# A two-block transformer kernel: input and norm columns laid out by the host, first two weight slabs taken together by pieces, and several waits and orders moved

## The reference, cut to what matters

```python
hn = rmsnorm(h, norm_mix_g[l])            # h = x, (256, 1024)
proj = hn @ w_in[l]                        # split into fq fk fv ff gq gf gi gg
fox_out = fox_attention(fq, fk, fv, log_sigmoid(ff + fox_f_bias))
rec = hgrn2_chunkwise(gq, gf, gi, lbs[l])  # linear recurrence, gated by gg
h = h + concat(fox_out, rec * ...) @ w_out[l]
mem_n = rmsnorm(mem, norm_mem_g[l])
h = h + memory_cross_attention(rmsnorm(h, norm_x_g[l]), mem_n, w_xq, w_xkv, w_xo)
h = h + square(relu(rmsnorm(h, norm_ff_g) @ w1)) @ w2
h = rmsnorm(h, final_norm_g)
```

## Time and profile before

| | us |
|---|---|
| median of 3 runs | 907.87 (906.85 to 908.96) |
| the profiled execution, whole | 906.91 |
| its span | 905.1 |
| TensorE busy in it | 890.8 (98%) |
| VectorE busy | 605.0 |
| ScalarE busy | 489.3 |

### The profile page before, as it was taken

How to read it: one execution, slowest core, us unless ns; L and a number is a source line. 1 busy time by engine, 2 the same in 40 slices (tenths; PEclk the granted TensorE clock), 3 DMA queues, 4 the chain that set the end, 5 groups by cost and what they waited for, 6 DMA issues and landing times.

```text
span 905.1 us, 15854 instructions
## 1 busy us (share of the span) xinstructions
PE 890.8 (98%) x6305; PEld 820.6 (91%) x6305; DVE 605.0 (67%) x812; ACT 489.3 (54%) x727; POOL 107.6 (12%) x136
## 2 busy tenths in 40 slices
PE   9999999899999999999999999999999999999997
PEld 8988987788988999988899989999999899999886
DVE  6795875755655766644467547898686688888643
ACT  7766545534655655433364336664644666666432
POOL 6431132200000100000026070001000100000000
PEclk9999999999999999999999999999999999999999
DMA  9958632234533866555547554345556486666641
GB/s 290 304 176 278 213 124 94 94 135 144 187 94 94 262 200 202 194 186 189 199 149 224 199 196 150 105 146 158 187 186 186 117 226 192 185 187 203 213 140 47
DMA packets 135266, 159.63 MB, mean 176 GB/s; under 512 B 3951, under 2 KB 113773, under 8 KB 134957
## 3 DMA queue, kind: packets, MB, share of 16 engines
q1 hardware_dynamic: 133261, 151.79, 52.4%
q0 software_dynamic: 1344, 6.03, 1.9%
q10 hardware_dynamic: 608, 1.06, 0.3%
HBM read 157.81 MB, written 1.05 MB: 176 GB/s over the span
## 4 chain that ended last, share of the span: by engine, by line
PE 86%; DVE 5%; ACT 3%; issue 3%; DMA 1%; SPq 1%; POOL 0%; DVEq 0%; POOLq 0%; ACTq 0%
PE tb L698 15%; PE tb L700 15%; PE tb L699 15%; PE acc L698 11%; PE acc L700 11%; PE acc L699 11%; DMA raw<-in_w_in 1%; PE acc L990 1%; ACT whi L1327 1%; DVE wlo L1863 1%; DVE wlo L1939 1%; PE tb L1084 0%; DVE dz L2017 0%; PE acc L1210 0%; PE tb L1066 0%
## 5 line engine op out<-in xcount | busy, mean ns | idle before, releaser
L1863 DVE TENSOR_TENSOR wlo<-raw,whi 128x2048 fp32r<-128x2048 f32 x138 | 317.1, 2301 | 187.6 <-ACT whi L1327 187.2
L1327 ACT ACTIVATE whi<-raw 128x2048 fp32r<-128x2048 f32 x138 | 264.1, 1915 | 183.9 <-PE acc L700 121.5
L698 PE MATMUL tb<-xhi,whi 128*128 128x256 f32 x1192 | 331.8, 278 | 2.1 <-DVEq L2002 1.2
L700 PE MATMUL tb<-xhi,wlo 128*128 128x256 f32 x1192 | 329.3, 276 | 0.0
L699 PE MATMUL tb<-xlo,whi 128*128 128x256 f32 x1192 | 329.3, 276 | 0.0
L698 PEld LDWEIGHTS tb<-xhi,whi 128*128 128x128 f32 x1192 | 223.8, 188 | 3.0 <-DVEq L2002 1.4
L699 PEld LDWEIGHTS tb<-xlo,whi 128*128 128x128 f32 x1192 | 223.9, 188 | 0.1
L700 PEld LDWEIGHTS tb<-xhi,wlo 128*128 128x128 f32 x1192 | 223.8, 188 | 0.0
L698 PE MATMUL acc<-whi,hid_hi 128*128 128x512 f32 x128 | 50.0, 390 | 0.0
L700 PE MATMUL acc<-whi,hid_lo 128*128 128x512 f32 x128 | 49.8, 389 | 0.0
L699 PE MATMUL acc<-wlo,hid_hi 128*128 128x512 f32 x128 | 49.8, 389 | 0.0
(11 more groups left out here) (408 smaller groups left out, 1524.2 us busy)
## 6 DMA issues: line engine op xcount, KB each, us to landing
raw<-in_w_in SPq DMA_DIRECT2D x37, 1024.0 KB, 5.2
raw<-in_w SPq DMA_DIRECT2D x32, 1024.0 KB, 5.4
raw<-in_w_up SPq DMA_DIRECT2D x44, 512.0 KB, 5.0
raw<-in_w_down SPq DMA_DIRECT2D x22, 512.0 KB, 4.1
raw<-in_w_xkv SPq DMA_DIRECT2D x8, 1024.0 KB, 6.3
raw<-in_w_out SPq DMA_DIRECT2D x8, 1024.0 KB, 4.9
raw<-in_w_mem_kv SPq DMA_DIRECT2D x4, 1024.0 KB, 5.1
raw<-in_w_xq SPq DMA_DIRECT2D x4, 1024.0 KB, 5.0
```

The source lines that it names most:

```text
L698: pe.matmul(o, a_hi, b_hi, start=start, stop=False)
L700: return pe.matmul(o, a_lo, b_hi, start=False, stop=stop)
L1327: act.activation(whi[:, n % RING, :m], raw[:, n % RING, :m], ACT.Copy).then_inc(hi_ready, 1)
L1863: dve.tensor_tensor(low(n), raw[:, n % RING, :m], whi[:, n % RING, :m].bitcast(F32), ALU.subtract).then_inc(lo_ready, 1)
```

## The change: the input and the norm columns from the host, a new opening, orders and waits moved

- The host lays out x transposed (`xT`), all small parameters as 128-row columns (`cols`), and the first six slabs as they lie in SBUF (`opening`, 8 KB per partition and slab). Two DMAs bring `cols` (64 B, later 952 B, per partition) in place of 15; PE's turning of x and of the columns goes, with `turn_x`.
- SP loads, for each of four g: x^T piece g (256 KB), piece g of slab 0, piece g of slab 1; then slab 2, then x (for the sums alone). ACT and DVE split x^T straight from SBUF (`x_hi`, `x_lo`), and PE takes slabs 0 and 1 together, piece by piece (`first_pair`).
- ACT: the sums of x come after both banks of slabs 0 and 1 are emptied and before the pieces of slab 3. The sums of `mem` and their load come later; `laid` of `mem` and `spread("mem")` move to `fv`. `spread("x")` moves from behind slab 2 to between the pieces of slab 3.
- Slab 6 gets bank 3 and waits for no bank. `lo` of slab 8 goes ahead of the scans on DVE, and slab 5's bank and `hi` of slab 8 ahead of ACT's Exp and Ln.
- Around heads 5 and 7, `vm`, `xo`, `plo` and `h4` the orders change as below.

```diff
-            load_x(0)
-            load_x(2)
-            load_piece(0, 0)
-            load_x(1)
-            load_x(3)
+            for g in range(4):
+                sp.dma_start(turned_x[:, 2 * g:2 * g + 2, :], w["xT"][:, 2 * g:2 * g + 2, :]).then_inc(xT_in[g], 16)
+                load_piece(0, g)
+                load_piece(1, g)
+            for p in range(PIECES[2]):
+                load_piece(2, p)
+            for q in range(4):
+                load_x(q)
...
-        X_BANK = {0: 0, 1: 1, 2: 2, 3: 0, 4: 1, 5: 0, 6: 1, 7: 0, 8: 1}
-        BANK_BEFORE = {3: 0, 4: 1, 5: 3, 6: 4, 7: 5, 8: 6}
+        X_BANK = {0: 0, 1: 1, 2: 2, 3: 0, 4: 1, 5: 0, 6: 3, 7: 0, 8: 1}
+        BANK_BEFORE = {3: 0, 4: 1, 5: 3, 7: 5, 8: 4}
...
+            def first_pair():
+                for p in range(4):
+                    for n in range(2):
+                        if p == 3:
+                            split_ready(n)
+                        else:
+                            pe.wait_ge(piece_hi, 2 * p + n + 1)
+                            pe.wait_ge(piece_lo, 2 * p + n + 1)
+                        pe.wait_ge(xs["lo"], p + 1)
+                        for c in range(2):
+                            for k in (2 * p, 2 * p + 1):
+                                last = mm3(o, a_hi[n][:, k, m], a_lo[n][:, k, m], XHI["x"][:, k, :], XLO["x"][:, k, :],
+                                           k == 0, k == 7)
...
                 empty_pair(A + j, dz[:, 0, d:d + T], dz[:, 0, d + T:d + 2 * T])
-                if j:
-                    act.wait_ge(mem_in, 16)
-                    sumsq("mem", xn)
+            for q in range(4):
+                act.wait_ge(x_in[q], 16)
+                sumsq("x", h, [q])
+            for j in range(2):
                 for p in range(2):
                     hi_piece(A + j + RING, p)
...
@@ ACT, 12 slabs
+                if i in (5, 7):
+                    fox_copy(i - 1)
+                if i == 5:
+                    hi(n + RING)
                 if i == 7:
-                    fox_copy(6)
+                    laid(turned_mem, C["norm_mem_2"], (2, 3))
+                    fox_exp(7)
+                    hg_exp(8)
+                    fox_hi(6)
@@ PE, 12 slabs, i == 7
                         emptied(first["xk"] + 3)
-                        emptied(first["xv"] + 3)
@@ DVE, 12 slabs
-                if i == 7:
-                    laid(turned_mem, C["norm_mem_2"], (2, 3), 4)
-                lo(n + RING)
-                if i == 7:
-                    hg_diff(8)
+                if i not in (7, 11):
+                    lo(n + RING)
                 if i < 8:
                     fox_mask(i)
+                    if i == 7:
+                        laid(turned_mem, C["norm_mem_2"], (2, 3), 4)
+                        hg_diff(8)
...
+                    if i == 7:
+                        lo(n + RING)
...
+                    dve.wait_ge(slab_done, n + 1)
+                    dve.tensor_scalar(vm[:, 1, :], acc[:, 0, 1, :], rs[:, NORM["mem2"], 1:2], None, ALU.mult).then_inc(vm_low, 1)
...
-            h4_lo(0, (0, 1))
+            h4_lo(0, (0,))
             summed("h4", 1)
+            h4_lo(0, (1,))
```

More of the change, by code:

```diff
@@ L467, in _ @@
-            load_x(2)
-            load_piece(0, 0)
-            load_x(1)
-            load_x(3)
[L471 to L477, removed]
+                sp.dma_start(raw[:, n % RING, cut], w["opening"][n, :, cut]).then_inc(landed_at, 16)
@@ L481, in _ @@
[L481 to L486, removed]
@@ L751, in row_slab @@
                             last.then_inc(part_done, 1)
-                last.then_inc(slab_done, 1)
+                if tiles[-1]:
+                    last.then_inc(slab_done, 1)
             def tile_slabs(n0, hi, lo, k0):
@@ L903, in _ @@
             A = first["gf"]
-            for n in range(A, first["fv"]):
+            first_pair()
+            for n in range(A + 2, first["fv"]):
                 if n in BANK_BEFORE:
                     emptied(BANK_BEFORE[n])
-                if n == 1:
-                    filled("x")
                 if n in PIECES:
@@ L912, in _ @@
                     t_slab(n, XHI["x"], XLO["x"], X_BANK[n])
[L913 to L927, removed]
+            emptied(2)
+            pe.wait_ge(spread_kept, 1)
             for j, name in enumerate(("fv", "gi", "gg")):
@@ L932, in _ @@
                     half_slab(first[name] + k, XHI["x"], XLO["x"], 4 * k, j % 2)
+                if name == "fv":
+                    spread("mem", tb[:, 2, :])
             def fox_scores(i):
@@ L1401, in hi_piece, with x_hi @@
                     .then_inc(hi_ready if p == PIECES[n] - 1 else piece_hi, 1)
[L1403 to L1408, removed]
+            def x_hi(g):
+                act.wait_ge(xT_in[g], 16)
+                for kt in (2 * g, 2 * g + 1):
+                    last = act.activation(XHI["x"][:, kt, :], turned_x[:, kt, :], ACT.Copy,
                                           scale=cols[:, C["norm_mix_g"] + kt:C["norm_mix_g"] + kt + 1])
-                last.then_inc(fil["hi"], 1)
+                last.then_inc(xs["hi"], 1)
             def empty_pair(n, one, two, scale=1.0):
@@ L1416, in empty_pair @@
                 act.activation(two, second_bank(n), ACT.Copy, scale=scale).then_inc(act_emptied, 1)
-            act.wait_ge(cols_ready, 1)
+            act.wait_ge(cols_in["first"], 16)
             for g in range(4):
-                turn_x(g)
+                x_hi(g)
                 hi_piece(0, g)
[L1422 to L1425, removed]
+                hi_piece(1, g)
             for p in range(2):
@@ L1476, in _ @@
             hi(n + RING)
+            act.wait_ge(mem_in, 16)
+            sumsq("mem", xn)
             for j in range(2):
@@ L1483, in _ @@
                 hi(n - 1 + RING)
+                if name == "fv":
+                    act.wait_ge(cols_ready, 1)
+                    act.wait_ge(memT_in, 16)
+                    laid(turned_mem, C["norm_mem_g"], range(4))
+                else:
+                    act.wait_ge(spread_made, 2)
+                    act.activation(factor_r, tb[:, 2, 0:T], ACT.Copy).then_inc(spread_kept, 1)
                 empty(n, dst[:, 0, :], ACT.Copy, acc[:, j, 0, :], scale=rs[:, NORM["x"], 0:1])
@@ L2039, in _ @@
             link(dve.tensor_scalar(small[:, 56:57], small[:, 56:57], -LAM_INIT, None, ALU.add))
-            lo(first["fq"] + 2 + RING)
-            laid(turned_mem, C["norm_mem_g"], range(4), 0)
-            for n in range(first["fq"] + 3, first["gg"] + 1):
+            for n in range(first["fq"] + 2, first["gg"] + 1):
                 lo(n + RING)
+                if n == first["fv"]:
+                    laid(turned_mem, C["norm_mem_g"], range(4), 0)
             def hg_diff(m):
```

160 lines of the change are left out of this document (75 added, 85 removed).

## The result

The changed kernel takes 902.23 us, the median of five runs (901.81 to 904.0); the kernel before took 907.87 (906.85 to 908.96). The ratio is 0.9945, 95% interval [0.9932, 0.9959]. Forecast were 901.3 and 898.0 to 904.5. The time is inside the range, 0.9 above 901.3, but the way to it is not the one forecast: the opening gave nothing, and the late edits gave more than forecast.

A forecast was written before the change was run, and what follows sets the result against it. PE, busy 98% of the span, was taken to bound the kernel; 2.0 us from the opening plus 4.05 from the late edits, 6.05 in all, gave a forecast of 901.3 us, range 898.0 to 904.5.

The forecast's parts named there:

- Opening, data: Start of the kernel: x^T and first pieces land early enough for a first matmul at 6.3 us, 2.5 earlier.
- First pair: Slabs 0 and 1 together: 10.9 us of matmuls plus 0.6 for a late second g, ending at 17.8.
- Slab 3: PE before slab 3: a new hole of 0.6 us (0 to 0.9) behind ACT's copies, sums and rounding.
- The DVE chain to slab 8: Slabs 5 to 8: lo 6 ends at 38.8, lo 7 at 45.4; new waits of 0.8 and 1.1, bank hole gone.
- the forecast hole at slab 10: PE before slab 10: lo 10 ends at 62.3 where PE wants it at 61.8, 0.4 us new.
- Late edits: Heads 5 and 7, vm, xo, plo and h4: reordering gains 4.05 us in all.
- head 7 with the spread: Head 7: PE's waits for the spread (0.7) and DVE's normalisation (1.8) go, 2.5 us gained, bounds 0.7 to 2.5.
- Head 7's third rival: Head 7: the hole only moves, to xv's bank or products behind POOL; 1.8 stays, 903.1 us; chance 0.08.
- h4: At h4: DVE's sum waits for ACT's sum of squares, so at most 0.25 of the 0.9 us hole goes.
- The sum: Whole kernel: 2.0 from the opening plus 4.05 from the late edits, 6.05 us gained.
- The first rival: Opening bound by late columns or pieces: pair ends at 19.1 to 19.7, its 2.0 gone, 903.3 us; chance 0.14.
- the fourth rival: Opening: a longer hole drops PE's clock to 1.2 GHz, matmuls cost 10.9 us more, 914 us; chance 0.05.

The follow-up runs named there:

- experiment 4: The changed kernel with two of ACT's four sums of squares of x ahead of its copies of the banks of slabs 0 and 1; 901.35 us, ratio 0.9941.
- experiment 5: The changed kernel with two x sums ahead of the bank copies, spread of x behind slab 2, SP's small loads behind slab 5; 900.48 us, ratio 0.9933.
- Experiment 3: The changed kernel with POOL's scaling of fq waiting until DVE's small operations are done; 903.12 us, ratio 0.9956.
- the opening alone: The changed kernel with the late edits put back, so only the opening differs from the kernel before; 909.1 us, ratio 1.0021.
- 7: The changed kernel with lo of slab 8 behind DVE's scans again; 903.81 us, ratio 0.9967.
- 9: The kernel of experiment 5 with POOL's load of mem issued behind the scaling of gq; 899.47 us, ratio 0.9919.
- 12: The kernel of 9 run once more, unchanged; 899.69 us, ratio 0.9929.

## Why the prediction was right in its time and wrong in its opening

**Opening, data.** Right but for one piece. The first matmul came at 6.52 (forecast 6.3). x^T piece 1 reached ACT at 7.91, 0.7 later than forecast, and ACT had waited 1.33 for it. The columns, issued at 0.82, landed 3.0 us later (ACT's first split is at 3.88), at the early end of the earlier trace rows.
The Trainium skill, "DMA: Bandwidth & Descriptors", section "Specifications", puts transfers below 512 B under line rate. In this trace the 8 KB load in runs of 64 B was not late: 3.0 us, where the quickest 256 KB piece of x^T took 2.9. Whether longer runs would have been quicker still, no run here shows.

**First pair.** Undersized, for x^T piece 1. The last matmul of the first g starts at 9.31, so the next was due at 9.42 and came at 10.47: a hole of 1.05 where 0.6 was forecast, and 0.89 is what the row calls idle. A matmul's record lasts 0.28 and the next starts 0.113 after it, so an idle time in PE's rows is a hole less about 0.17. Another 0.2 went in the first matmuls, which start more slowly (6.52, 6.80). The pair ends at 18.75 (forecast 17.8). Slab 3 then starts at 25.09: its hole is 0.9, at the upper bound of the forecast (0.6, from 0 to 0.9).

**The DVE chain to slab 8.** This is the step that failed. It had `lo` 5 ending at 33.7, `lo` 6 at 38.8, `lo` 7 at 45.4; measured are 34.89, 40.37 and 47.95. Of the 2.6 at the end, 1.2 were there at `lo` 5, 0.4 came on the way to `lo` 6 and 1.0 on the way to `lo` 7. Two causes:
- ACT reached slab 5 late (1.2). Its rounding stands behind the norm factor, which came at 28.55, after a wait of 0.74 for PE's spread; this stood behind the first piece of slab 3, and slab 3 behind ACT's sums. I had the sums and the spread in the walk, each too early. I had also priced SP's queue at nothing and did not walk slab 4's load: it landed at 26.6, behind SP's small loads, and ACT waited 2.02 for it. In after the spread came later still; in experiment 4, with the sums earlier, the load comes last (a wait of 2.61 for it, none for the spread). Experiment 4 took 0.9 back by the sums alone, experiment 5 another 0.9 by spread and loads together; how that divides is not shown.
- DVE beside POOL (0.4 and 1.0). The 128x8 operation took 1.20 where it had 0.76 in before, and 0.15 in experiment 5, where POOL was idle then. The pair on `dz` behind `lo` 6 took 1.79; in before, with POOL idle, it had 0.73 (timeline of DVE, before). From `lo` 6 to `lo` 7 it is 7.62 where I took 6.57 from the earlier trace rows, though POOL's work falls elsewhere now. Experiment 3 shows that one wait on POOL does not escape it.

```profile
39.44 0.73 DVE L1987 TENSOR_SCALAR dz<-dz,small 128x256 f32<-128x256 f32 x2
```

Because PE was as late as before at slab 9 (59.15 against 59.00), the forecast hole at slab 10 did not come, and `spread("mem")` cost its whole 0.61 where I had 0.3. Net at the end of the projections: -0.6 in place of +2.0.

**Late edits.** The mechanisms were right, and the sizes too small by 1.2. Differences of the table of instructions: heads 5 and 6, 0.45 (forecast 0.4 for head 5); head 7 with the spread, 2.67 (2.5); then 0.44 up to `dz` for the 0.2 wait for `am` in front of the recurrence, which I had not summed; `vm` 0.49 (0.5); the cross attention 0.55 (0.2); from there to `h4`, `plo` among it, 0.44 (0.2); `h4` 0.25 (0.25). The waits that went are 4.3 us in the rows. The 1.0 more lies in four places, 0.2 or 0.3 each: head 7, the wait for `am`, the cross attention and `plo`; at heads 5 and 6, `vm` and `h4` the rows gave the whole. What makes the difference is not shown. Head 7's third rival is refuted: no wait stands before these rows of PE and DVE in after, and the normalisation ends at 175.83.

```profile
176.28 0.49 PE L942 MATMUL tb<-ident,fs 128*128 128x128 f32 x3
```

```profile
174.42 1.41 DVE L2074 TENSOR_SCALAR fs<-fs,rden 128x256 f32<-128x256 f32 x1
```

**h4.** Right: the wait is 0.64 where it was 0.88, because DVE's sum now waits 0.18 for ACT's sum of squares, not for its own list.

```profile
711.81 0.21 DVE L2409 TENSOR_SCALAR rs<-ss 128x1 f32<-128x1 f32 x1 [0.18 <-ACT junk L1782]
713.02 0.71 PE L1279 MATMUL tb<-dg,h 128*128 128x128 f32 x4 [0.64 <-DVE dg L2422]
```

**The sum.** 2.0 + 4.05 = 6.05 was forecast; -0.61 + 5.24 = 4.63 is what the profiled executions differ by. Two errors, 2.6 too much in the opening and 1.2 too little in the late edits, cancel in part, and that the median came within 0.9 of the forecast is luck. The range did not need it: the opening's error alone gives 903.9, which 898.0 to 904.5 holds too. The medians differ by 5.6, 1.0 more than the profiled executions. That fits the clock falling in some runs of the kernel before, whose traced execution, at 1.00, lies below its median; for these five runs it is not shown. The first rival gave the time of the opening nearly (903.3), but with data as its cause; beyond the 0.7 of x^T piece 1 it was ACT and DVE. Of the fourth rival the mechanism exists. In the opening alone it set in after a hole no longer than the one I took for harmless; there it lasted about 4 us and cost about 1.7, not 10.9.

## What to carry to other kernels

When an engine is made to start earlier, sum the work of the engines that feed it over the whole stretch, not only over the first step: here DVE was busy 13.6 of 14 us, in before and in after alike, so PE could start 2.3 us earlier and arrive no earlier. Walk every load that is queued behind the ones that moved, and look for large transfers beside the tight ones. Look at the granted clock of every run before taking a hole for harmless from one trace. Price a hole of PE from the starts on both sides of it, not from the idle time of its row, and check a sum by instructions that both traces share, or two errors can pass for a right answer.

## What the runs showed of the hardware that I had not expected

- A hole of 1.77 to 1.85 us in PE was followed by a granted clock of 0.50 in one profiled execution; holes of 1.76 (before), 1.94 (after) and 1.85 (experiments 3 and 7) in other executions were not.
- Runs of the kernel before with a mean granted clock of 0.996 or 0.997 have a median of 908.0 us, those with 0.999 or 1.000 one of 906.5.
- Two simultaneous 1 MB loads: slab 6's took 9.3 us beside `mem` (experiment 5); without it the loads of that stretch took at most 6.1 (9) and 7.1 (12).
- DVE beside POOL: a 128x8 multiplication took 1.20 beside it and 0.15 without it and a pair of 128x256 operations 1.79 and 0.73. The POOL operation beside the second took no longer than usual (1.30).
